# A two-layer mixing network on one core: five reorderings around its mix layers and the seam between them

## What is computed

```python
for l in range(DEPTH):                       # DEPTH = 2
    h = einsum('bsd,dc->bsc', x, w_in[l])
    a_q, a_k, a_v, b_q, b_k, b_v, i_q, i_k, i_w, c_q, c_kv, c_kr = split_cols(h)
    o_a = sliding_window_sink_attn(rope(a_q), rope(a_k), a_v, attn_sinks[l])
    o_b = indexer_sparse_attn(rope(b_q), rope(b_k), b_v, rope(i_q), rope(i_k), i_w)  # the 64 best keys of each query
    o_c = mla_attn(...)                      # latent: from c_q, c_kv, c_kr
    x = layer_norm(ALPHA * x + concat([o_a, o_b, o_c]) @ w_out[l])
    x = layer_norm(ALPHA * x + moe_ffn(x))
# moe_ffn: one of 4 groups of 4 experts is chosen per token, two experts in it, with
# shares w; h = silu(x @ w_gate) * (x @ w_up) * share; y = sum over experts of h @ w_down
```

## Time and profile before

| what | value |
|---|---|
| runs, median (lowest to highest) | 1168.52 us (1166.01 to 1171.72), 3 runs |
| profiled execution | 1168.65 us, span 1167.2 us |
| PE busy | 1117.7 us (96%) |
| DVE busy | 895.2 us (77%) |
| ACT busy | 741.7 us (64%) |
| mean granted clock of PE | 0.993 |
| second network, first mix layer | from about 575 us |
| gather of the first layer's experts | 702.66 us |
| seam between the layers | 862 to 884 us |
| gather of the second layer's experts | 999.24 us |

### The profile page before, as it was taken

One profiled execution on the slowest core, in us unless ns is written; L12 is line 12 of the kernel. 1 busy time (PEld: TensorE's weight loads), 2 busy tenths in 40 slices (PEclk: granted clock), 3 DMA queues, 4 the chain that ended last, 5 costly groups with the idle time before them and its releaser, 6 DMA issues.

```text
span 1167.2 us, 14667 instructions
## 1 busy us (share of the span) xinstructions
PE 1117.7 (96%) x5515; PEld 914.2 (78%) x5515; DVE 895.2 (77%) x1462; ACT 741.7 (64%) x1313; POOL 0.2 (0%) x4
## 2 busy tenths in 40 slices
PE   7999999999999999998999999999989999999996
PEld 5788787888787788887877787877778778787774
DVE  4756857777768867766668868999977886899996
ACT  5746565655656665556355556888845655688883
POOL 0000000000000000000000000000000000000000
PEclk9999999999999999999999998999999999999998
DMA  8654454453443455633542416999926322499991
GB/s 288 239 181 144 145 177 137 157 179 109 145 140 114 164 197 172 201 108 106 184 145 108 145 38 190 348 360 359 360 91 214 130 99 87 157 357 357 364 349 39
DMA packets 131841, 221.25 MB, mean 190 GB/s; under 512 B 6144, under 2 KB 77360, under 8 KB 131760
## 3 DMA queue, kind: packets, MB, share of 16 engines
q1 hardware_dynamic: 127920, 213.21, 53.2%
q10 hardware_dynamic: 3840, 6.98, 1.8%
HBM read 219.13 MB, written 1.05 MB: 189 GB/s over the span
## 4 chain that ended last, share of the span: by engine, by line
PE 74%; DVE 14%; ACT 7%; issue 3%; DMA 2%; ACTq 0%; DVEq 0%
PE bank L487 20%; PE bank L489 20%; PE bank L488 20%; PE bank L786 3%; PE bank L851 3%; DVE wL L440 2%; ACT wH L432 2%; ACT S L806 2%; DMA ring<-in_w_mem_kv 1%; PE bank L636 1%; PE bank L2277 1%; PE bank L832 1%; DVE mx L795 1%; PE bank L2326 1%; PE bank L1738 1%
## 5 line engine op out<-in xcount | busy, mean ns | idle before, releaser
L440 DVE TENSOR_TENSOR wL<-ring,wH 128x1024 fp32r<-128x1024 f32 (+1 forms) x316 | 375.9, 1213 | 138.5 <-ACT wH L432 137.3
L432 ACT ACTIVATE wH<-ring 128x1024 fp32r<-128x1024 f32 (+1 forms) x316 | 320.5, 1047 | 32.3 <-PE bank L489 19.8
L487 PE MATMUL bank<-wH,hTH 128*128 128x512 f32 (+2 forms) x592 | 237.9, 402 | 3.0 <-DVE wL L440 2.1
L488 PE MATMUL bank<-wL,hTH 128*128 128x512 f32 (+2 forms) x592 | 232.1, 392 | 0.0
L489 PE MATMUL bank<-wH,hTL 128*128 128x512 f32 (+2 forms) x592 | 231.9, 392 | 0.0
L487 PEld LDWEIGHTS bank<-wH,hTH 128*128 128x128 f32 x592 | 111.5, 188 | 27.9 <-DVE wL L440 3.5
L489 PEld LDWEIGHTS bank<-wH,hTL 128*128 128x128 f32 x592 | 111.5, 188 | 24.8
L488 PEld LDWEIGHTS bank<-wL,hTH 128*128 128x128 f32 x592 | 111.6, 189 | 23.1 <-issue 0.5
L487 PE MATMUL bank<-wH,xgH 128*128 128x512 f32 x256 | 105.2, 411 | 0.0
L488 PE MATMUL bank<-wL,xgH 128*128 128x512 f32 x256 | 101.9, 398 | 0.0
L489 PE MATMUL bank<-wH,xgL 128*128 128x512 f32 x256 | 101.9, 398 | 0.0
(11 more groups left out here) (297 smaller groups left out, 1863.0 us busy)
## 6 DMA issues: line engine op xcount, KB each, us to landing
ring<-in_w_in_a SPq DMA_DIRECT2D x44, 1024.0 KB, 4.9
ring<-in_w_out SPq DMA_DIRECT2D x20, 1024.0 KB, 4.8
ring<-in_w_down SPq DMA_DIRECT2D x20, 1024.0 KB, 6.3
ring<-in_w_gate SPq DMA_DIRECT2D x36, 512.0 KB, 5.1
ring<-in_w_up SPq DMA_DIRECT2D x36, 512.0 KB, 6.5
ring<-in_w_in_b SPq DMA_DIRECT2D x14, 1024.0 KB, 5.0
ring<-in_w_mem_kv SPq DMA_DIRECT2D x8, 1024.0 KB, 7.1
ring<-in_w_in SPq DMA_DIRECT2D x8, 1024.0 KB, 5.4
```

Of the source, the lines that this page charges most:

```text
L432: act.e.activation(quarter_parts(q)[0], quarter_in_ring(q), COPY).then_inc(w_high, 1)
L440: dve.e.tensor_tensor(lo, quarter_in_ring(q), hi.bitcast(F32), SUB).then_inc(w_low, 1)
L487: pe.e.matmul(o, a[0], b[0], start=first, stop=False)
L488: pe.e.matmul(o, a[0], b[1], start=False, stop=False)
```

## The change

Five edits. (1) In the second layer `second_tile` is called before the first chunk of tile 1, at (1, 0), no longer before chunk 6 of tile 0, at (0, 6); in the first layer it stays. (2) In the latent units the turning of the queries moves from `between(3)` to `between(4)`, on PE and ACT. (3) Of the eight rounds for tile 1, two per unit for n = 1 to 4 before, now one stands behind the scores of n = 1, 2, 3, two of n = 4, and one each in `between` at 3, 5 and 7, behind Y. (4) `slot_gates` is split by group: group g's part stands behind the up products of expert 4g, with a bank and a DVE copy of four columns of its own. (5) More zeros: 12 to 14 and 5 to 8 in each mix layer, 10 to 14 at the end of layer 0's experts.

```diff
@@ pe_proj_by_tiles
-        def pe_proj_by_tiles(name, meanwhile):
+        def pe_proj_by_tiles(name, meanwhile, place):
...
-                    if i == 0 and kk == 6:
+                    if (i, kk) == place:
                         meanwhile()
@@ pe_mix_layer
-            pe_proj_by_tiles(f"h{l}0", second_tile)
+            pe_proj_by_tiles(f"h{l}0", second_tile, (1, 0) if l else (0, 6))
...
-                if n == 3:
+                if n == 4:
                     pe_flip(("qT3", l), chunk(HR), 4, [at("queries", l)])
...
-            pe_idle(12, att_bank(("idle", l, 2), None))
+            pe_idle(14, att_bank(("idle", l, 2), None))
...
-            pe_idle(5, att_bank(("idle", l, 3), None))
+            pe_idle(8, att_bank(("idle", l, 3), None))
@@ dve_mix_layer
                 if 0 < n < 5:
-                    best(1, 2)
+                    best(1, 2 if n == 4 else 1)
...
+                if n in (3, 5, 7):
+                    best(1, 1)
@@ pe_few
-            def slot_gates():
-                b = att_bank((*way, "gates"), at(*way, "slot_gate"))
+            def slot_gates(g):
+                b = att_bank((*way, "gates", g), at(*way, "slot_gate", g))
                 pe.wait_ge(at(*way, "gates"))
-                for g in range(4):
-                    for i in range(2):
-                        mm = pe.e.matmul(b.t[:, 4 * g:4 * g + 4], OH[:, i, g * P:(g + 1) * P].bitcast(F32), SG[:, i, 4 * g:4 * g + 4], start=i == 0, stop=i == 1)
-                mm.then_inc(*pe.did(*way, "slot_gates"))
+                for i in range(2):
+                    mm = pe.e.matmul(b.t[:, 0:4], OH[:, i, g * P:(g + 1) * P].bitcast(F32), SG[:, i, 4 * g:4 * g + 4], start=i == 0, stop=i == 1)
+                mm.then_inc(*pe.did(*way, "slot_gates", g))
...
+                if e % 4 == 0:
+                    slot_gates(g)
                 if e:
                     down(e - 1)
-                else:
-                    slot_gates()
...
-                pe_idle(10, att_bank((*way, "idle"), None))
+                pe_idle(14, att_bank((*way, "idle"), None))
@@ dve_few
-                if e == 0:
-                    dve.wait_ge(at(*way, "slot_gates"))
-                    dve.e.tensor_copy(slot_gate, bank_of[(*way, "gates")].t[:, 0:16]).then_inc(*dve.did(*way, "slot_gate"))
+                if e % 4 == 0:
+                    g = e // 4
+                    dve.wait_ge(at(*way, "slot_gates", g))
+                    dve.e.tensor_copy(slot_gate[:, e:e + 4], bank_of[(*way, "gates", g)].t[:, 0:4]).then_inc(*dve.did(*way, "slot_gate", g))
```

## The result

The changed kernel is slower. Its median is 1177.28 us (1174.62 to 1179.99, 8 runs); the kernel before took 1167.18 us (1165.44 to 1171.72, 8 runs) beside it. The ratio is 1.0076, with a 95% interval of 1.0056 to 1.0095. The forecast was 1172 us, 0.3% more, so its sign held and its size did not: the time lies 0.3 us above the upper end of the range, and by the bound of 0.5% that the text set itself this is "slower", for which it had a chance of 0.20. The profiled execution of the changed kernel took 1179.99 us, the longest of its eight. Its page begins as follows (span and shares of the chain that ended last, as in the earlier trace rows).

A forecast was written before the change was run, and what follows sets the result against it. TensorE bounds the kernel, with 74% of the chain that ended last. Seam 3.8, queries 0.1, rounds -0.6, shares 1.4 and first layer -1.5 sum to +3.2 us, hence 1172 us; range 1166 to 1177, holding 8 in 10.

The forecast's parts named there:

- The seam: Between the layers: PE waits for L440 until 876.57, then six matmuls, turning and shift product follow; +3.8 us.
- the term "2.4 us": Seam, ACT: time from the shift product's copy (882.5) to slab h11's first cut (884.9), taken from the trace before.
- The bounds (+2.2 to +5.0): Seam's cost: +2.2 us with the clock high throughout, +5.0 with it low through turning and shift product.
- The queries: Mix layers: the 0.99 us wait goes, gain 0.2, loss 0.25 at L1815; +0.1 us for both layers.
- bounds -0.6 and +0.6: Range of the queries' term in the mix layers, around +0.1 us; the lower end is 0.29 us each.
- rival A: Clock falls at more places, the seam and expert 1's start: sum +9.2 us, 1178 us, slower; chance 0.15.
- The rounds: Windowed units: the 0.84 us PE wait goes, most returns at the chosen unit; -0.6 us over two layers.
- I get 666.1: First chosen unit: DVE's maximum, at 665.92 before, starts no earlier despite the moved rounds.
- The shares: Experts, second layer: about 0.2 us gained at expert 0, three groups give back 1.6 us; +1.4 us.
- Rival D: Narrow passes are hidden in the experts' stretch, limited by DVE's 19.43 of 20 us: 1169 us; chance 0.08.
- The zeros and the first layer: Gather to expert 0: zeros cost nothing, first layer runs like the second; -2.9 - 0.2 + 1.6 = -1.5 us.

The follow-up runs named there:

- queries with bank and zeros: Kernel before plus the queries' edit, one PSUM bank left out of the rotation and four zeros ahead of L1815: 1168.17 us, ratio 0.9986.
- the last kernel: Kernel before plus more zeros, queries' edit with bank left out and four zeros, h10's fourth weight quarter cut earlier, and seam's edit: 1166.09 us, ratio 0.9971.
- the two of the early cut: Kernel before with h10's fourth weight quarter cut ahead of the first exit tile's copies: 1166.86 us; the same plus the seam's edit: 1168.03 us.

## Why the prediction was right and wrong

**The seam: mechanism right, size a little small.** The wait ended by L440 (4.77 us) and the order behind it were as told. Measured +4.4 for +3.8. The missing part is the term "2.4 us" from the shift's copy to the next cut: from copy to cut it was 3.4 us (884.45 to 887.85), with one DMA issue of 1.91 us in it, so that PE then waits 0.96 us at slab h11 and 0.59 us at L1727. The reference was also a poor one: of nine traces without edits at the seam, four (queries alone, queries with bank and zeros, rounds alone, shares alone) had the clock high behind the shift product, and there the seam took 24.0 to 24.1 us; the other five, the profile of before among them, had it low and took 25.5 to 26.9. Against the first the edit, with the clock low for 3.4 us in it, costs 6 us. The bounds (+2.2 to +5.0) took both ends from the clock behind the edit and none from the clock before it.

**The queries: the step that failed.** The text had the wait nearly right ("one of about 1.2 us at L1815", measured 1.33) and its direct cost too (nothing, where the clock stays). What failed is the line "bounds -0.6 and +0.6": the edit joins two waits, 0.99 and 0.29, into one of 1.33, and behind that the clock fell in four of six layers, at 3.3 us or more each. The prediction saw at the seam that the clock falls behind waits of 1.21 and 1.60 us, and at the experts' start behind shorter ones, and put rival A on these two places. It did not put the same question to the wait that it had itself forecast. A's number, 1178 us, is right; its condition, a clock below 1.00 at 718 to 723 us in both layers, is not: there it was 1.00. So that number came near by luck, with falls at another place.

**The rounds: wrong sign.** "I get 666.1" for the chosen unit's maximum was wrong by nearly the full round; it started 1.1 us later, 0.9 when counted from the first L943. The prediction took the round away ahead of a Y where DVE itself waited for PE, 0.53 us, a row it had not read. Measured +0.45 us a layer with the clock high, for -0.3, and 1.6 more where the clock fell behind the longer wait at the chosen unit (1.2 us for 0.61).

**The shares: right place, a size too high.** The start gained 0.2 us in the second layer, as told. Three groups gave back 0.22 us each and not 0.57: the price per pass was taken from sixteen in a row, and in a stretch where DVE was busy 19.43 of 20 us the rest may have been hidden, which no run shows by itself. Rival D would then have had the mechanism, halfway. Second layer +0.5 for +1.4.

**The zeros and the first layer: right, in part by the choice of the trace.** -3.1 us from gather to turning came as worked out, and with the zeros alone it was -2.9. But it needed a trace of before in which the clock had fallen twice in the first layer, which only two other kernels' traces show; and how much of it is owed to the zeros and how much to the passes is open.

Put together, in the two profiled executions: seam +4.4, clock and rounds in the mix layers +8.1, shares and zeros -1.9, against +3.8, -0.5 and -0.1.

## What to carry to other kernels

When an edit joins two short waits of TensorE into one, or makes the wait it leaves longer than those behind which the clock falls elsewhere in the same trace, price that fall (here 3 to 5 us each in the mix layers) before the tenths won by it; the rotation of PSUM banks is one place that makes such a wait, and one bank left out unmakes it. Where a kernel's clock falls in some executions and not in others, read several traces before a forecast takes a stretch from one. Before work is moved out of the way of a step, look whether the engine that does it waits there anyway. Before a product is moved ahead of its neighbours, look which of its operands comes last, and move that first.

## What was unexpected of the hardware

The granted clock fell to 0.50 and stayed there for the whole of 641 to 650 us and 945 to 954 us though PE shows no gap in them, and in two executions (after, with the seam put back, and the shares alone) for some 13 us; here the first of these:

```profile
641.00:654.00 13.00, 13.00 (x38) 9.70 (x37) 8.40 (x22) 5.98 (x22) 0.00 (x0) 0.50 0.00 1
```

Whether it falls differs from layer to layer of one execution (queries alone, above) and, by the mean granted clock, from execution to execution of one kernel (0.978 to 0.994 in the same kernel's ten), which is why a single profile of before was a poor ruler. The Trainium skill says (TensorE: Matmul & The Clock Gate, Part 1: The HAM clock gate) that the monitor's window runs free and does not restart with the kernel, so that the point of change varies between runs; these figures agree that it varies. The same page (section A second HAM failure mode: psum-queue depth-cycling) tells of a kernel whose small idle times, as it goes through its banks, were enough to bring the clock down and up again. The 1.33 us at L1815 comes from the rotation of banks too, but it is a single wait in a layer, with a fall behind it in 4 of 6.

Second, ACT's four DMA issues at the seam. In eleven of the fourteen traces one of them took 0.82 to 1.95 us and the other three 0.34 to 0.53, and it was not always the same one: 0.92 us before, 1.91 after, 1.95 in the last kernel. In the other three traces, the two of the early cut among them, all four stayed at 0.60 or less. What holds it up no run here shows. It stands ahead of the cut that slab h11 waits for, so it is worth about 1 us of the seam.
